# Own buffers for the first adaLN tiles, VectorE's copies in the paged units, and a unit's outputs turned within the late chunk

## The chip, the cores and the metric

One core of one Trainium2 chip runs the whole program in one launch. The metric is the device time of that launch in microseconds. A run gives one time; the profiled execution also gives a span, from the first to the last instruction of the program.

## The reference

Two decoder layers work on a prompt of 256 tokens and on 8 decoding sequences of 8 tokens with 1024 cached positions each (320 tokens, model width 1024, fp32). Cut to one layer:

```python
def run_layer(x, c, ...):
    sh, sc, g = adaln(c, w_ada_mix_l, b_ada_mix_l)      # silu(c) @ w + b, split in three
    h = x * (1 + sc) + sh
    o, state = mixer(split_heads(h @ w_in_l))
    x = layer_norm(DN_ALPHA * x + (1 + g) * (o @ w_o_l), ln1_g_l, ln1_b_l)
    sh, sc, g = adaln(c, w_ada_mlp_l, b_ada_mlp_l)
    h = x * (1 + sc) + sh
    f = jnp.square(jax.nn.relu(h @ w_up_l)) @ w_down_l
    x = layer_norm(DN_ALPHA * x + (1 + g) * f, ln2_g_l, ln2_b_l)
    return x, state
```

The mixer has three head groups: A (6 heads, dilated windows over a dense cache), B (6 heads, attention to the top 64 or 256 keys that an indexer of 8 small heads chooses, over a paged cache) and C (4 heads, the difference of two softmaxes, paged). A table of relative positions is added to the logits of all three.

## The kernel before, in words

**Tiles.** All weights but the indexer's own key matrix come as tiles of 128 x 1024 fp32 (512 KB). `STREAM` lists them in the order of use, `PLACE` gives each its number n, and tile n goes into slot n % 4 of `ring`. SyncE's `load` (L469) waits until tile n - 4 has been used (`tile_used`) and then issues one DMA.

**The front.** An adaLN row block is made from 4 tiles: `ada_tile` (PE, L1030) multiplies silu(c) by them into one PSUM bank, `ada_out` (ScalarE, L753) copies the bank to `adarow`, `ada_turn` (PE, L1040) transposes it, `ada_add` (VectorE, L1492 and on) adds groups and bias and writes `adaT`. `FIRST` is the shift (16 tiles' first half) and then the scale of layer 0, in order. After all 16 tiles VectorE makes h of the prompt (L1604, 8 instructions) and GpSimd h of the samples, and PE makes the indexer's queries: `by_chunks` (L1017, two tiles), two tiles by `chunk` (L1008), then keys and weights (L1084). On the way PE also makes a table of biases (L1060) that ScalarE stores to DRAM (L759), to be read back 16 times over by the bias loads. SyncE and ScalarE issue the 64 page loads of the indexer's cached keys (L489 and L774, 8 of 64 KB for each sequence); for each sequence the page numbers are read into registers first.

**Projections.** `PROJ` alternates dense tiles (8 of `feat`, 8 of `v`) with pairs of adaLN tiles. The indexer's scores come in between (`beside`), and from the seventh dense tile on VectorE takes the samples' top-k, 8 values at a time (`take8`: MAX8 L1593 and MATCH_REPLACE8 L1595), 32 times a layer.

**Attention.** 16 units follow: unit n is sequence n % 8, the first 8 with groups A and C, the last 8 (`second`) with B and C. Keys and values have two buffers each in `big`, so unit n + 2 is loaded when unit n is done with them: keys after its logits, values after its outputs. In a first unit the cache is 4 DMAs of 768 KB and 16 pages of 64 KB; in a second unit 8 + 8 pages of 192 KB and 8 + 8 of 64 KB, of which ScalarE issues the C keys (L873, 8) and SyncE the others (L489). Beside the units run 16 `item`s of the prompt's attention, about one per unit (`SLOTS`).

Within unit n PE does `turn(n)` (L1211, then a wait for `u_out` of unit n - 1, then L1220), `logits(n+1)` (L1192, in second units L1198 too), the item's transposes (L1280) and logits (L1265), `values(n)` (L1235), the item's outputs (L1290), a late weight chunk (L1008, in units 0 to 6), and `turn_out(n)` (L1242). ScalarE copies the turned weights out of PSUM (`turned_unit` L882 and L884, `turned_item` L901) and takes the exponentials (L840, L842, L893). VectorE reads logits (L1649, L1713), scales the unit's outputs (L1686 to L1690), scales the item (L1724, L1728), copies the item's outputs (L1742), takes one `take8`, puts the unit's outputs away (`place_outputs`, L1700, which signals `u_out`), and takes the other `take8` (units 0 to 6). After the 32nd, VectorE writes `sel` (L1782), for which the logits of unit 8 wait.

All orders are written by hand; nothing is scheduled by a planner.

## Time and profile before

| | us |
|---|---|
| runs shown, median (lowest, highest) | 1428.89 (1428.22, 1435.41) |
| the profiled execution's own time | 1424.0 |
| its span | 1422.2 |
| PE busy | 1298.5 (91%) |
| VectorE busy | 517.4 (36%) |
| ScalarE busy | 286.5 (20%) |
| GpSimd busy | 60.0 (4%) |
| moved by DMA | 363.79 MB, mean 256 GB/s |

In the table by stretch of time each engine has its busy time and, in brackets, its count of instructions; then come the share of full speed that TensorE's clock was granted and the mean busy share of the 16 DMA engines, where 1.00 and more is an engine set with no gap. In the timeline a row is a start, a length, engine and line, and in square brackets the engine's idle time before it with what ended it. SPq and ACTq are queues that issue DMAs. PEld is the weight load of PE.

### The profile page before, as it was taken

What the parts mean: (1) busy time and instruction counts of PE and PEld (TensorE: products, weight loads), DVE (VectorE), ACT (ScalarE), POOL (GpSimd) and SP (SyncE); (2) the same over time, 40 slices, a digit from 0 to 9 for tenths busy, and PEclk for the clock granted to TensorE, in tenths of its full rate; (3) what the DMA queues carried; (4) which work ended last, traced back from release to release, by engine and by line L of the source; (5) the groups of instructions that cost most, each with busy time, mean ns of one, the idle gap of its engine ahead of it and who ended that gap; (6) DMA issues with size and microseconds to landing.
All of it is one profiled execution on the core that took longest, in us unless ns stands there. A gap on an engine that the chain in (4) does not pass through costs nothing.

```text
span 1422.2 us, 23165 instructions
## 1 busy us (share of the span) xinstructions
PE 1298.5 (91%) x8038; PEld 814.3 (57%) x8038; DVE 517.4 (36%) x1350; ACT 286.5 (20%) x713; POOL 60.0 (4%) x265
## 2 busy tenths in 40 slices
PE   5789798878699999999999999998789999999998
PEld 1444255544466666666665544665456667767775
DVE  1102688865255111111113079777534611100113
ACT  0111123333223101100004112433322310100001
POOL 1100000000001000000001000000000100000000
PEclk9899999999899999999999999999979999999999
DMA  8778979999954667887864587999995446675663
GB/s 303 211 264 269 295 238 350 371 275 307 313 194 141 218 229 272 297 307 278 299 226 162 209 278 240 314 371 324 300 326 189 172 185 222 215 278 209 225 224 133
DMA packets 189565, 363.79 MB, mean 256 GB/s; under 512 B 22912, under 2 KB 140360, under 8 KB 187786
## 3 DMA queue, kind: packets, MB, share of 16 engines
q1 hardware_dynamic: 165200, 350.19, 71.9%
q10 hardware_dynamic: 24250, 12.14, 3.3%
q8 instruction: 64, 1.05, 0.3%
q14 instruction: 51, 0.42, 0.1%
HBM read 354.17 MB, written 58.40 MB: 290 GB/s over the span
## 4 chain that ended last, share of the span: by engine, by line
PE 70%; SPq 9%; DMA 7%; DVE 5%; issue 4%; DVEq 2%; ACT 2%; ACTq 0%
PE psf L1008 24%; PE psf L1424 19%; SPq L489 8%; DMA ring<-in_tiles 6%; PE psf L1300 4%; PE psf L1339 3%; PE psf L1407 3%; PE psf L1030 2%; PE psf L1235 2%; PE psf L1192 2%; PE psf L1079 1%; DVE m L1593 1%; DVEq L1596 1%; PE psf L1334 1%; PE psf L1105 1%
## 5 line engine op out<-in xcount | busy, mean ns | idle before, releaser
L1008 PE MATMUL psf<-hT,ring 128*128 128x320 f32 x1440 | 402.0, 437 | 11.1 <-DMA ring<-in_tiles 7.8
L1008 PEld LDWEIGHTS psf<-hT,ring 128*128 128x128 f32 x1440 | 271.5, 191 | 141.1 <-issue 14.7
L1424 PE MATMUL psf<-big,ring 128*128 128x320 f32 x1024 | 278.7, 433 | 3.8 <-DVE big L1811 2.1
L1424 PEld LDWEIGHTS psf<-big,ring 128*128 128x128 f32 x1024 | 193.5, 190 | 89.9 <-issue 5.8
L1811 DVE TENSOR_TENSOR big<-sq 128x320 f32<-128x320 f32 x64 | 31.5, 492 | 248.4 <-ACT sq L977 248.1
L1508 DVE TENSOR_SCALAR rstd<-psf,adaT 128x256 f32<-128x256 f32 x32 | 15.4, 482 | 248.9 <-PE psf L1424 233.7
L1192 PE MATMUL psf<-big,qs 128*32 128x512 f32 x512 | 74.6, 671 | 8.0 <-issue 5.6
L935 ACT ACTIVATE sq<-xT 128x320 f32<-128x320 f32 x32 | 15.0, 470 | 321.0 <-DVE xT L1512 321.0
L1593 DVE MAX8 m<-workbuf 64x8 f32<-64x1032 f32 x64 | 78.5, 1227 | 3.0
L1030 PE MATMUL psf<-ring,cz 128*32 128x512 f32 x384 | 61.8, 633 | 19.3 <-DMA ring<-in_tiles 10.7
L1595 DVE MATCH_REPLACE8 workbuf<-m,workbuf 64x1032 f32<-64x1032 f32 x64 | 77.4, 1209 | 0.0
L1235 PE MATMUL psf<-big,ptbuf 128*32 128x128 f32 x2048 | 66.1, 283 | 11.1 <-DMA big<-in_pool_cv 10.3
L977 ACT ACTIVATE sq<-psf 128x320 f32<-128x320 f32 x64 | 28.0, 437 | 238.9 <-PE psf L1008 224.5
L1300 PE MATMUL psf<-oT,ring 128*128 128x320 f32 x256 | 71.6, 435 | 2.1 <-DVE oT L1700 1.0
L1235 PEld LDWEIGHTS psf<-big,ptbuf 128*32 128x32 f32 x2048 | 57.2, 114 | 18.0 <-issue 16.2
L1649 DVE CUSTOM_DVE_ANT_0 S<-psf,sbias 128x1032 f32<-128x1032 f32 x32 | 39.4, 1233 | 60.4 <-PE psf L1198 54.6
L1300 PEld LDWEIGHTS psf<-oT,ring 128*128 128x128 f32 x256 | 47.8, 190 | 23.4 <-DVE xT L1512 1.7
L1339 PE MATMUL psf<-ring,hT 128*128 128x512 f32 x128 | 60.3, 615 | 0.0
L794 ACT ACTIVATE zT<-psf,zscale 128x320 f32<-128x320 f32 x40 | 20.7, 527 | 166.4 <-PE psf L1008 129.6
L1492 DVE TENSOR_REDUCE adaT<-psf 128x36 f32<-128x144 f32 x24 | 7.3, 304 | 117.3 <-PE psf L1040 116.8
L1220 PE MATMUL psf<-ident,S 128*128 128x128 f32 x128 | 22.4, 302 | 24.8 <-DVE oT L1700 24.3
L1407 PE MATMUL psf<-hT,big 128*128 128x320 f32 x128 | 38.3, 464 | 3.1 <-ACT hT L952 3.1
(183 smaller groups left out, 1158.8 us busy)
## 6 DMA issues: line engine op xcount, KB each, us to landing
ring<-in_tiles SPq DMA_DIRECT2D x284, 512.0 KB, 4.5
big<-in_cache_a SPq DMA_DIRECT2D x64, 768.0 KB, 7.2
out_cache_a<-in_cache_a SPq DMA_DIRECT2D x64, 768.0 KB, 5.8
big<-in_pool_bk SPq DMA_DIRECT2D x128, 192.0 KB, 3.7
big<-in_pool_bv SPq DMA_DIRECT2D x128, 192.0 KB, 4.6
big<-in_pool_cv SPq DMA_DIRECT2D x256, 64.0 KB, 4.3
big<-in_pool_ck SPq DMA_DIRECT2D x128, 64.0 KB, 4.4
big<-in_pool_ck ACTq DMA_DIRECT2D x128, 64.0 KB, 4.6
```

Of the source, the lines that this page charges most:

```text
L489: sp.dma_start(dst[:, j, :], pool[ds(at[j] + l * N_PHYS, 1), :, w0:w0 + dst.shape[2]] .rearrange("o p w -> (o p) w")).then_inc(signal, 16)
L1008: ins = pe.matmul(ps[:, 0:T], ring[:, s, k, :], rhs[:, k, :], start=k == 0, stop=k == KD - 1)
L1030: ins = pe.matmul(bank[3][G * g:G * g + G, :], cz[:, c, :], wide(s, kk), start=c < 4, stop=c >= 4)
L1192: ins = pe.matmul(psf[G * c:G * c + G, 512 * q:512 * q + w], qs[:, u.s, G * c:G * c + G], rhs, start=True, stop=not masked)
L1235: ins = pe.matmul(bank[3][G * c:G * c + G, 0:P], lhs, rhs, start=j == 0, stop=j == NPG)
L1300: ins = pe.matmul(wo_bank(m)[:, 0:T], ring[:, s, k, :], oT[:, AT_O[k], :], start=k == 0, stop=k == KD - 1)
L1339: ins = pe.matmul(bank[v_bank(g, tt)], hT[:, 2 * s + kk, P * tt:P * tt + P], wide(slot, kk), start=first, stop=last)
L1407: ins = pe.matmul(up_bank(m)[:, 0:T], spare[m][:, k, :], hT[:, k, :], start=k == 0, stop=k == KD - 1)
L1424: ins = pe.matmul(bank[6 + m % 2][:, 0:T], ring[:, s, k, :], uT[:, KD * q + k, :], start=q + k == 0, stop=q == 3 and k == KD - 1)
L1593: dve.max(m8[0:TS, 0, :], work)
L1595: dve.match_replace(work, m8[0:TS, 0, :], work, TAKEN)
L1649: dve.tensor_tensor_reduce(out=S[:, 0, :], in0=psf[:, 0:L], in1=sbias[u.second][:], scale=1.0, scalar=-3e38, op0=ALU.add, op1=ALU.max, acc ...
```

## The change

**Front.** `FIRST` takes the four groups of 4 tiles in the order 0, 2, 1, 3, so that shift and scale of chunks 0 to 3 come first. Only its first 4 tiles use the ring; the other 12 have buffers of their own (`ahead`, in `big` and in `zT`, both free then) and are issued without a wait. x goes behind 8 tiles, the four tiles of the indexer's queries go next into the ring, then the last 8 of FIRST. `ring_at` renumbers the slots. PE does half of the queries (chunks 0 to 3) behind the eighth tile and the other half behind the sixteenth; the bias table moves behind the twelfth. VectorE, GpSimd and ScalarE are put in the matching order, the small constants get two semaphores, and the indexer's page loads move: sequences 0 and 1 on SyncE ahead of the constants, 2 and 3 between the first projection tiles, and on ScalarE one sequence less at the start and one more behind the first tiles.

**A unit's outputs.** In units 0 to 6 `turn_out` stands between the halves of the late chunk, `place_outputs` stands ahead of both `take8`s. In units 7 to 14 `place_outputs` stands ahead of `item_out`. In units 13 and 14, which have another item, `turn_out` goes ahead of its steps.

**Paged units.** In the second units VectorE does the copies of `turned_unit` and `turned_item`, and ScalarE issues 4 of the 8 C value pages (`load_c_values`), behind a wait for the outputs of unit n.

```diff
-FIRST = some("mix", 0, 0, 16)
+FIRST = [t for q in (0, 2, 1, 3) for t in some("mix", 0, 4 * q, 4 * q + 4)]
...
+        ahead = [x.rearrange("p (k m) -> p k m", k=KD)
+                 for m in range(6) for x in (big[:, KD * P * (4 + m):KD * P * (5 + m)],
+                                             zT[:, :, :].rearrange("p z t -> p (z t)")[:, KD * P * m:KD * P * (m + 1)])]
...
+        def ring_at(t):
+
+            n = PLACE[t]
+            return n if n < RING else n - len(FIRST) + RING
...
             sp.dma_start(cT[:], a["cond"]).then_inc(ld_cond, 16)
-            for t in FIRST[:12]:
+            for t in FIRST[:RING]:
                 load(t)
+            for m in range(4):
+                load_ahead(m)
             sp.dma_start(xT[:], a["x"]).then_inc(ld_x, 16)
-            for t in FIRST[12:]:
+            for t in INDEX[0]:
                 load(t)
+            for m in range(4, 12):
+                load_ahead(m)
...
                     sp.wait_ge(ld_first, N_FIRST)
-                    load_ik(l, 0)
+                    for b in range(2):
+                        load_ik(l, b)
...
                     load(t)
+                    if l == 0 and n in (1, 3):
+                        load_ik(l, 2 + n // 2)
...
-                    load_c(l, then, was, 1)
+                    load_c(l, then, was, 1, range(NPG // 2 if then.second else NPG))
...
             for n, t in enumerate(FIRST):
                 ada_tile(t)
-                if n == 3:
+                if n == 4:
+                    pe.wait_ge(ld_begin, N_BEGIN)
+                    ada_turn(0)
+                if n in (7, 11):
+                    ada_turn(n // 4)
+                if n == 7:
+                    for m, q in enumerate(INDEX[0]):
+                        part_of_queries(m, q, range(KD // 2))
+                if n == 11:
                     pe.wait_ge(ld_first, N_FIRST)
...
-                    by_chunks(l, 0, INDEX[l][:2], in_bank)
-                    for m in range(2, 4):
-                        chunk(INDEX[l][m], in_bank(m), hT)
+                    for m, q in enumerate(INDEX[l]):
+                        part_of_queries(m, q, range(KD // 2, KD)).then_inc(tile_used, 1)
...
-                        chunk(MID[l][u.n + 1], late_bank(u.n + 1), hT)
+                        late = MID[l][u.n + 1]
+                        part_of_chunk(late, late_bank(u.n + 1), range(KD // 2))
+                        turn_out(u)
+                        part_of_chunk(late, late_bank(u.n + 1), range(KD // 2, KD)).then_inc(tile_used, 1)
+                    else:
+                        turn_out(u)
                     for k in slots[1:]:
                         item_turn(k - 1)
                         item_logits(k)
-                    turn_out(u)
-                    for k in slots[1:]:
                         item_outputs(k - 1)
...
+                    if NB <= u.n + 2 < UNITS:
+
+                        act.wait_ge(u_o.sem, u_o.done(l, u.n))
+                        load_c_values(UNIT[u.n + 2], was)
...
                 for u in UNIT[:-1]:
                     n, slots = u.n, SLOTS[u.n]
+                    if u.second:
+                        turned_unit(u)
                     read_logits(UNIT[n + 1])
+                    if u.second:
+                        turned_item(slots[0] - 1)
                     item_read(slots[0])
                     read_outputs(u)
                     item_scale(slots[0])
+                    if n + 1 >= len(LATE):
+                        place_outputs(u)
                     if slots[0]:
                         item_out(slots[0] - 1)
+                    if n + 1 < len(LATE):
+                        place_outputs(u)
...
-                    while taken < upto - 1:
-                        take8()
-                        taken += 1
-                    place_outputs(u)
```

On PE, at the start of the program, the order before is this (L1030 adaLN tiles, L1040 their transposes, L1017 and L1008 the queries, L1084 the indexer's keys):

```order
L1040 MATMUL psf<-ident,adarow 128x128 x4
L1030 MATMUL psf<-ring,cz 32x512 x8
L1040 MATMUL psf<-ident,adarow 128x128 x4
L1030 MATMUL psf<-ring,cz 32x512 x6
L1040 MATMUL psf<-ident,adarow 128x128 x4
L1017 MATMUL psf<-hT,ring 128x320 x16
L1008 MATMUL psf<-hT,ring 128x320 x16
L1084 MATMUL psf<-hT,wki 72x320 x8
L1008 MATMUL psf<-hT,ring 128x320 x8
```

In the same place it is now (L1073 adaLN tiles, L1083 transposes, L1103 the queries, L1120 the bias table, L1140 the indexer's keys, L1056 the first projection):

```order
L1083 MATMUL psf<-ident,adarow 128x128 x4
L1103 MATMUL psf<-hT,ring 128x320 x16
L1073 MATMUL psf<-big,cz 32x512 x2
L1073 MATMUL psf<-zT,cz 32x512 x2
L1073 MATMUL psf<-big,cz 32x512 x2
L1073 MATMUL psf<-zT,cz 32x512 x2
L1083 MATMUL psf<-ident,adarow 128x128 x4
L1120 MATMUL psf<-big,relb 16x512 x2
...
L1083 MATMUL psf<-ident,adarow 128x128 x4
L1103 MATMUL psf<-hT,ring 128x320 x16
L1140 MATMUL psf<-hT,wki 72x320 x8
L1056 MATMUL psf<-hT,ring 128x320 x8
```

The first 16 of the queries' 32 matrix products now stand ahead of the last 8 adaLN tiles, and the bias table behind four of these.

On PE, within unit 1 of a layer, from the unit's last value product on, it was (L1242 is `turn_out`, L1220 the transposes that wait for `u_out`):

```order
L1235 MATMUL psf<-vs,ptbuf 32x128 x4
L1290 MATMUL psf<-adarow,vp 64x128 [waits i_tset]
L1290 MATMUL psf<-adarow,vp 64x128
L1008 MATMUL psf<-hT,ring 128x320 [waits ld_w2,i_logit]
L1008 MATMUL psf<-hT,ring 128x320 x7
L1242 MATMUL psf<-turnO,osb 128x64 [waits u_oset]
L1211 MATMUL psf<-ident,S 128x128 [waits u_exp,u_tset]
L1211 MATMUL psf<-ident,S 128x128 x3
L1212 MATMUL psf<-ident,znew 64x128
L1220 MATMUL psf<-ident,S 128x128 [waits u_out]
```

and is now:

```order
L1363 MATMUL psf<-hT,ring 128x320 [waits ld_w2,i_logit]
L1363 MATMUL psf<-hT,ring 128x320 x3
L1298 MATMUL psf<-turnO,osb 128x64 [waits u_oset]
L1363 MATMUL psf<-hT,ring 128x320 [waits ld_w2]
L1363 MATMUL psf<-hT,ring 128x320 x3
L1267 MATMUL psf<-ident,S 128x128 [waits u_exp,u_tset]
L1267 MATMUL psf<-ident,S 128x128 x3
L1268 MATMUL psf<-ident,znew 64x128
L1276 MATMUL psf<-ident,S 128x128 [waits u_out]
```

`turn_out` moved ahead by half a chunk, and so stands farther from the transposes that wait for what comes of it.

On VectorE, at the start of unit 8, the first paged unit, the order now is (L1839 and L1841 are `turned_unit`, L1724 the logits of unit 9, L1849 `turned_item`):

```order
L1839 COPY ptbuf<-psf 64x128 [waits u_o,u_tp]
L1841 COPY ptbuf<-psf 128x512 x2
L1724 ISA S,mx<-psf,sbias 128x1032 [waits u_s,u_tp]
L1724 ISA mx 128x1
L1727 TENSOR_SCALAR nmx<-mx 128x1
L1849 COPY adarow<-psf 128x512 [waits i_o,i_tp]
L1788 ISA S,mxi<-psf,pbias 128x128 [waits i_s,i_tp]
```

Before, the row of L1649 (now L1724) was the unit's first on VectorE and L1713 (now L1788) followed its two helpers; the four copies stood on ScalarE.

## Rows read from the trace of the kernel before

**Rows 1.** Windows: stretch, length, busy (count) by engine, PE clock, DMA share, GB/s.

```profile
0.00:38.60 38.60, 20.32 (x86) 4.73 (x86) 7.46 (x30) 4.03 (x7) 5.67 (x18) 0.95 0.84 306
38.60:68.70 30.10, 23.32 (x80) 15.28 (x80) 2.93 (x7) 3.07 (x7) 3.40 (x10) 0.90 0.74 189
68.70:100.00 31.30, 27.51 (x108) 15.32 (x108) 0.46 (x3) 3.29 (x6) 0.00 (x0) 0.89 0.84 276
212.00:300.00 88.00, 76.87 (x856) 50.05 (x858) 72.81 (x196) 31.29 (x90) 6.78 (x36) 0.99 1.03 353
300.00:305.00 5.00, 5.00 (x103) 3.14 (x95) 2.34 (x8) 1.62 (x4) 1.13 (x6) 0.88 0.33 96
320.00:377.00 57.00, 42.08 (x571) 26.08 (x571) 25.08 (x101) 20.94 (x61) 4.52 (x24) 0.91 1.01 313
377.00:403.00 26.00, 22.16 (x265) 14.84 (x269) 9.21 (x39) 9.60 (x26) 0.00 (x0) 0.87 0.81 265
895.00:980.00 85.00, 76.10 (x858) 50.13 (x861) 68.04 (x192) 32.00 (x93) 6.78 (x36) 1.00 1.05 361
980.00:990.00 10.00, 8.16 (x141) 5.02 (x137) 6.17 (x25) 3.41 (x11) 1.13 (x6) 1.00 0.84 248
```

**Rows 2.** Timeline of PE, 0 to 100 us.

```profile
13.48 2.12 PE L1060 MATMUL psf<-big,relb 34*16 34x512 f32 x6 [1.26 <-DMA zscale<-in_zscale]
...
23.20 1.05 PE L1030 MATMUL psf<-ring,cz 128*32 128x512 f32 x4 [1.27 <-DMA ring<-in_tiles]
24.50 1.05 PE L1030 MATMUL psf<-ring,cz 128*32 128x512 f32 x4 [0.24 <-DMA ring<-in_tiles]
...
36.17 0.66 PE L1040 MATMUL psf<-ident,adarow 128*128 128x128 f32 x4 [0.70 <-ACT adarow L753]
38.63 10.40 PE L1017 MATMUL psf<-hT,ring 128*128 128x320 f32 x32 [1.80 <-DVE hT L1604]
48.86 8.78 PE L1008 MATMUL psf<-hT,ring 128*128 128x320 f32 x32
57.48 4.47 PE L1084 MATMUL psf<-hT,wki 128*72 128x320 f32 x16
68.73 6.41 PE L1008 MATMUL psf<-hT,ring 128*128 128x320 f32 x16 [6.79 <-DMA ring<-in_tiles]
...
91.32 1.05 PE L1030 MATMUL psf<-ring,cz 128*32 128x512 f32 x4 [3.09 <-DMA ring<-in_tiles]
```

**Rows 3.** Timeline of PEld and VectorE, 0 to 40 us.

```profile
11.17 0.14 PEld L1030 LDWEIGHTS psf<-ring,cz 128*32 128x32 f32 x4 [0.98 <-DMA ring<-in_tiles]
...
37.54 3.99 DVE L1604 TENSOR_SCALAR hT<-xT,adaT 128x256 f32<-128x256 f32 x8
```

**Rows 4.** Timeline of SyncE's queue, 35 to 70 us.

```profile
40.48 11.96 SPq L489 DMA_DIRECT2D big<-in_pool_ik  x8
```

**Rows 5.** Waits, 205 to 296 us (layer 0, units 0 to 7): total, times, longest.

```profile
PE psf L1220 <- DVE oT L1700: 4.5, 4, 2.0
```

**Rows 6.** Waits, 296 to 405 us (layer 0, units 8 to 15).

```profile
PE psf L1220 <- DVE oT L1700: 8.4, 7, 2.8
...
PE psf L1235 <- DMA big<-in_pool_cv: 6.4, 2, 4.7
```

**Rows 7.** Waits, 975 to 1085 us (layer 1, units 8 to 15).

```profile
PE psf L1235 <- DMA big<-in_pool_cv: 3.9, 2, 2.5
```

**Rows 8.** Groups by shape, VectorE's and ScalarE's: busy us, mean ns, idle before.

```profile
L1664 DVE COPY workbuf<-psf 64x512 f32<-64x512 f32 x4 | 2.8, 688 | 11.2 <-PEq L1119 11.1
...
L884 ACT ACTIVATE ptbuf<-psf 128x512 f32<-128x512 f32 x64 | 34.0, 582 | 0.0
```

**Rows 9.** VectorE, 296 to 405 us: its groups by shape, then its timeline.

```profile
L1742 DVE COPY oT<-psf 64x128 f32<-64x128 f32 x18 | 5.1, 286 | 0.2
...
313.05 1.23 DVE L1649 CUSTOM_DVE_ANT_0 S<-psf,sbias 128x1032 f32<-128x1032 f32 x1 [3.50 <-PE psf L1198]
```

**Rows 10.** Timeline of SyncE's queue, 356 to 402 us.

```profile
369.35 4.02 SPq L489 DMA_DIRECT2D big<-in_pool_cv  x8
```

205 lines of the change are left out of this document (126 added, 79 removed).

## The prediction, made before the changed kernel was run

> **What bounds the kernel now.** I read the windows first, since the whole-span shares hide that three places have three limits. The reader is to look at the last two columns, DMA share and GB/s. In the front the 16 DMA engines are busy 0.84, 0.74 and 0.84 of three stretches that cover 0 to 100 us; in the units of layer 0 the share is 1.03 over 88 us and in the paged units 1.01, and the same of layer 1 (1.05) [rows 1]. So in the attention DMA sets the pace and in the front it should, but doesn't. Then the timeline of PE over the front. Three things stand there. From 17 to 30 us every adaLN product waits for its tile: starts at 23.20 and 24.50, 1.30 apart, each only 1.05 long [rows 2]. From 36 to 62 us the work is PE's own, in a row: h, 10.40, 8.78, 4.47 [rows 2]; the DMA share falls to 0.74 there because the four ring slots hold the tiles in use. And at 68.73 PE has stood 6.79 us for the first projection tile, then runs it at 6.41 [rows 2]. The queue of SyncE tells why: its eight page loads of one sequence took 11.96 us to issue, from 40.48 to 52.44 [rows 4], with the constants, another eight and the first projection tiles behind them. Last the waits in the units: PE stood for `place_outputs` 4.5 us in units 0 to 7 and 8.4 us in units 8 to 15 [rows 5, 6], and for C values 6.4 us there [rows 6] and 3.9 us in layer 1 [rows 7].
>
> **The sum is made against the profiled execution's own 1424.0 us** (span 1422.2). The median of the runs shown is 4.9 above it, so 4.9 is added at the end.
>
> **Front, the tiles.** The third ring tile behind the first came in at 11.17 [rows 3]. From there at 1.30 a tile, twelve buffers of their own, no wait: the eighth tile (4 more) at 16.4, x, 1280 KB or 2.5 tiles, at 19.6, the four query tiles from 20.9 to 24.8, the last of the 16 at 24.8 + 8 x 1.30 = 35.2.
>
> **Front, PE.** Behind the eighth tile: its product 1.05, the copy to `adarow` 0.58 (ScalarE's 582 ns for 128 x 512 out of PSUM [rows 8]), the transposes 0.66, VectorE's add, taken at 0.5, and the first chunk of h, 3.99 / 8 = 0.5 [rows 3], so the queries begin near 20.1, by when x is in. Half of the queries is half of 10.40 + 8.78, taken warm at 8.8; the last two of the four query tiles come at 23.5 and 24.8, ahead of their use. So to about 29. Then four adaLN products, 4.2, copy 0.6, transposes 0.66 and the bias table 2.12 [rows 2]: 37 to 38, by which all tiles are in (35.2). Four products 4.2 to 41.9; copy, transposes, add and h with nothing beside them, 0.6 + 0.66 + 0.5 + 0.5, to 44.2; the second half 8.8 to 53.0; keys 4.47 to 57.5. Before, that chain ended at 57.48 + 4.47 = 61.95. **4.5 us** of PE's own chain go: the adaLN pieces between the halves are paid, the idle tile waits aren't.
>
> **Front, the first projection.** The query tiles' slots come free only with the second half (about 46 to 53), but slots 0 to 3 hold just those four: the first projection tile needs the first query tile's slot, so it leaves at about 47 and has 10 us to land. A 512 KB tile at the pace above is 1.3, and SyncE's page loads now stand in front of it, two sequences (16 issues; at the worst rate seen 24 us, at the rate of another eight, 4.02 us [rows 10], 8 us). They are issued right behind the last ahead tile at about 25 to 30, long before 47, where nothing on SyncE waits for a slot. Two more sequences stand between projection tiles, 4 to 12 us of issuing each in front of the third and fifth tile; the low end keeps a loss of that kind. I take the wait of 6.79 as gone, and with it the cold chunk: 6.41 against 8.78 / 2 = 4.39 warm, 2.0. So far 4.5 + 6.8 + 2.0 = 13.3. At 91.32 PE waited 3.09 for an adaLN tile [rows 2]; with the queue ahead of it relieved perhaps all of it goes and about 1.5 of slower products behind, 4.6: 17.9 in all.
>
> **What caps it.** DMA work does not shrink. 38.6 x 0.84 + 30.1 x 0.74 + 31.3 x 0.84 = 81 us of work stand in the first 100 [rows 1]. At a share of 0.97, about 83.6 us: at most 16.4 can go. At its start the queue is empty and can't reach that share. I take **14** for the front; low end 7 (only the chain's 4.5 and half the cold and waiting time less a new queue wait), high end 17.
>
> **Front, edits at nothing.** The smaller first semaphore (`ld_begin`), the lambda exponential moved behind the second copy, h in halves on GpSimd: all run beside tile waits. The bias table's store leaves ScalarE about 42 instead of about 20; the bias loads that wait for it stand behind the fourth projection tile on SyncE, due past 60. If that cover is gone, every tile behind that wait is late by the store's own length.
>
> **Units 0 to 7.** `turn_out` half a chunk (about 2.2 us) earlier removes what stood as 4.5 us in four waits [rows 5]. Moved are one transposition pair on PE and two copies on VectorE; the two `take8` ahead of which they now stand are late by these copies, 2 x 0.286 us at most, the row of a copy four times as wide [rows 9], and the last of them frees `sel`, for which unit 8's logits wait: 0.6 once a layer. But the DMA share there is 1.03 [rows 1]: a unit that ends 0.6 us earlier frees its keys earlier, and the transfer for n + 2 is still queued behind others. What is real is the gap: at 300 to 305 the share is 0.33, 0.67 x 5 = 3.35 us of empty DMA [rows 1], where unit 8 waits for `sel` and the keys and values of 9 and 10 can't leave. An earlier end of unit 7 moves the whole gap, and shortens it only if DMA finished its queue earlier too. Bounds: 0 and 4.5.
>
> **Paged units.** Per unit VectorE gets one small copy, 0.286 [rows 9], and two of 128 x 512, 2 x 0.688, together 1.66 us, and the item's, between 0.286 and 0.688 by its width, 0.55 in the mean; that size on VectorE is not in the trace with 128 partitions, the nearest row is 688 ns for 512 elements of 64 partitions; ScalarE took 582 [rows 8]. They stand in front of VectorE's read of the next logits, ahead of which it now stands idle for 3.50 us, waiting for PE's logits [rows 9]; 1.66 fits in there, so they are covered; the item's copy is in front of nothing that is ready. ScalarE gives up about 2 us of copies and gets four issues, 4.02 / 8 = 0.50 each [rows 10], 2.0 us, at a wait for `u_o`. Queued behind this wait is only the next unit's exponentials, not ready before. SyncE loses the same 2.0 us of 16 issues, eight of which took 4.02 [rows 10]. The share of 1.01 over 320:377 gives nothing to win; from 377 to 403 it is 0.81 [rows 1], an empty 0.19 x 26 = 4.9 us, with the longest C value wait, 4.7 [rows 6], in it. There half of the pages leave earlier: 2 to 3 us. With a share of the 3.35 at the gap, and about 1 to 2 of the units' own waits, **6** for layer 0 (0 to 13).
>
> The Trainium skill, *DMA: Bandwidth & Descriptors*, "Issuing engines are not separate DMA queues", says that DMAs started by several engines run on the same 16 and save the starting time of the sequencer only. By it the four issues that move to ScalarE are worth nothing where the trace shows a share of 1.01, and at most 4 x 0.5 us a unit in the tail. The trace of before agrees as far as it goes: cache loads already leave from two queues and the share is not above that of units with one.
>
> **Layer 1.** Share 1.05 over 85 us, then a gap of 0.16 x 10 = 1.6 us [rows 1], C value waits 3.9, longest 2.5 [rows 7]. I take **3** (0 to 6).
>
> **Sum.** 14 + 6 + 3 = 23: 1424.0 − 23 = 1401.0, and 4.9 for the median, **1406**.
>
> **Rivals.**
> (a) *Only the front counts*: the attention is DMA's in both layers, and PE merely waits for keys instead of for `u_out`. For it: shares of 1.03, 1.01, 1.05. Against: the gap at 300 and the tail at 377. 14 to 15: about **1414**.
> (b) *The front gives half*: page loads, constants and the bias store now share the saturated engines with the ahead tiles; at 11.96 for eight issues [rows 4], two sequences would hold SyncE up to 24 us, from 30 to 54, and the first projection tile, free at 47, leaves at 54. The 6.8 is then still about half there. 7 + 9 for the units: about **1413**.
> (c) *More*: the front at its cap 17 and the units' waits really gone, 4.5 + 3 in layer 0's first units, 5 in its tail, and half as much in layer 1, 33: about **1396**.
> (d) *The change does not do what it says*: ahead tiles land later since 12 tiles compete with page loads, x and constants; the halves each wait, and nothing within 0.5% remains: **1426**.
> (e) *Slower: VectorE's copies come on the path of the paged units.* PE transposes, VectorE copies, and PE's values can't start till then. If VectorE is still in the earlier unit's `item_out`, `place_outputs` or a top-k step, the copies end behind the logits. It decides from the point where that idle time ahead of the read, 3.50, is under the copies' own 1.66: then 14 units x (1.66 + 0.55) = 31 us are on the path, less 14 of the front: about **1446**. Against it: VectorE is busy 25 of 57 us there [rows 1].
> The Trainium skill, *VectorE: DVE Perf Modes*, "The TRN2 errata", has a table by which a copy of 512 out of PSUM takes (120 + 512) cycles at 0.96 GHz, 658 ns, on VectorE and (172 + 512) at 1.2 GHz, 570 ns, on ScalarE. The rows, 688 and 582, say the same with a little more: the engine to which the copies move is the slower one for them. That speaks against this part, and it matters only in (e).
>
> **Chances.** Forecast 0.56, (a) 0.17, (b) 0.10, (c) 0.07, (d) 0.06, (e) 0.04. A measurement of this kernel can tell about 0.5%, 7.1 us, from no change: faster than 1421.8 are the forecast, (a), (b) and (c), 0.90; same (d), 0.06; slower (e), 0.04. The range leaves out (d) and (e), and a tenth more on its two sides: 1393 to 1420. Its low end is all terms at their high ends (17 + 13 + 6 = 36), its high end the front's low end of 7 with 2 for the units.
>
> **What would show it.** The first projection chunk starts at 57 to 60 instead of 68.73 and has no long DMA wait; if it waits still for a ring tile behind page loads, (b). PE's waits for `place_outputs` shrink to under 1 us in units 0 to 7; if then waits for keys grow by as much, (a). The DMA share in the five us ahead of unit 9 rises from 0.33, and the longest C value wait falls from 4.7. VectorE's copies in the paged units end before PE's logits do; if a wait of the value products for VectorE stands among the waits with 1 us and more a unit, (e). The front's DMA share is 0.95 over 10 to 60 us. I am wrong if the share there stays at 0.8 with every tile in a buffer of its own, or if the stage between 100 and 212 us, which I left alone, stretches by what the front gave.

## The result and the profile after

| | before | after |
|---|---|---|
| median of the runs (lowest, highest), us | 1429.41 (1428.22, 1435.41) | 1408.67 (1405.41, 1411.64) |
| span of the profiled execution, us | 1422.2 | 1409.6 |
| VectorE busy, us | 517.4 | 550.2 |
| ScalarE busy, us | 286.5 | 258.1 |
| mean rate of DMA, GB/s | 256 | 258 |

The ratio (time of the changed kernel over that of before) is 0.9846, with a 95% interval of 0.981 to 0.9882: 22 us less (0.0154 x 1429; the two medians are 20.7 apart), where 23 was forecast. A second measurement of the same kernel gave 0.9854 (0.9821 to 0.9887). The two profiled executions are only 12.6 us apart: of before the profiled one was a quick one. A single trace stands for its kernel's median to about 5 us here, and in the runs below to about 8. Below, us of a part are always (1 − ratio) x 1429; the intervals are about 4 us to either side.

The forecast had 14 us for the front and 9 for the units. The parts measured alone (next section) came out otherwise, and the profile after already hints at it. The timeline of PE in the front of the changed kernel (start, length, engine and line, idle time before in brackets; L1103 queries, L1140 the indexer's keys, L1056 projection tiles):

```profile
24.01 8.85 PE L1103 MATMUL psf<-hT,ring 128*128 128x320 f32 x32 [1.88 <-DVE hT L1547]
...
42.99 10.54 PE L1103 MATMUL psf<-hT,ring 128*128 128x320 f32 x32 [1.80 <-DVE hT L1547]
53.37 4.47 PE L1140 MATMUL psf<-hT,wki 128*72 128x320 f32 x16
59.97 6.26 PE L1056 MATMUL psf<-hT,ring 128*128 128x320 f32 x16 [2.13 <-DMA ring<-in_tiles]
...
77.83 7.60 PE L1056 MATMUL psf<-hT,ring 128*128 128x320 f32 x16 [5.61 <-DMA ring<-in_tiles]
```

Against [rows 2] the first projection tile starts at 59.97 instead of 68.73 after a wait of 2.13 instead of 6.79. The wait at 91.32 is gone, but one of 5.61 stands at 77.83. Why the tiles were late is in the queue of SyncE, same kernel (L499 own-buffer tiles, L519 page loads, L584 constants, L493 ring tiles):

```profile
26.75 15.12 SPq L519 DMA_DIRECT2D big<-in_pool_ik  x16
41.92 4.76 SPq L584 DMA_DIRECT2D ident<-in_ident  x1
46.72 4.67 SPq L584 DMA_DIRECT2D onesd<-in_onesd  x1
...
55.59 1.06 SPq L493 DMA_DIRECT2D ring<-in_tiles  x2
59.68 3.96 SPq L519 DMA_DIRECT2D big<-in_pool_ik  x8
63.69 0.90 SPq L493 DMA_DIRECT2D ring<-in_tiles  x2
67.44 4.33 SPq L519 DMA_DIRECT2D big<-in_pool_ik  x8
...
72.23 0.36 SPq L493 DMA_DIRECT2D ring<-in_tiles  x1
```

The first projection tile leaves at 55.59, not at 47 as the prediction had it, since two constants took 4.7 us each to issue; the fifth leaves at 72.23, behind page loads, though the tile whose slot it takes was used by 66.2. The first of the two waits comes back in a second trace of the same kernel, the second only in part:

```profile
61.66 7.52 PE L1056 MATMUL psf<-hT,ring 128*128 128x320 f32 x16 [3.01 <-DMA ring<-in_tiles]
...
77.72 6.24 PE L1056 MATMUL psf<-hT,ring 128*128 128x320 f32 x16 [2.55 <-DMA ring<-in_tiles]
```

What filled the DMA engines meanwhile shows in the windows of the kernel after (length, busy by engine, PE clock, DMA share, GB/s) and in ScalarE's queue, first of before, then of after:

```profile
40.00:45.00 5.00, 2.67 (x8) 1.87 (x9) 3.25 (x13) 0.48 (x1) 1.64 (x4) 0.80 0.89 123
45.00:50.00 5.00, 5.00 (x17) 3.38 (x17) 0.62 (x5) 0.00 (x0) 0.00 (x0) 0.85 0.99 105
```

```profile
35.53 0.68 ACTq L759 DMA_DIRECT2D dist_sample<-big  x1
```

```profile
39.89 0.67 ACTq L795 DMA_DIRECT2D dist_sample<-big  x1
```

A share of 0.99 at 105 GB/s is the bias table's store: 16 partitions x 16 repeated rows of 4.6 KB, 1.19 MB. From 42 to 46 us of this trace the store's queue took 97% of the engines' time for 0.40 MB in 87 packets, so of 4.6 KB each; the page loads that run at 350 GB/s in the units have packets of 0.9 KB. Small packets are thus not what makes the store slow, and no run shows what does. It ran ahead of the constants before, and runs into them now. What it ran beside before were page loads: the 11.96 us for eight in [rows 4], which the prediction used as a worst rate, stand mostly under it (it landed at 50.4) and beside 16 page loads of ScalarE.

In the units, PE's waits for `place_outputs` in units 0 to 7 are gone, and another has come. The waits of PE from 205 to 292 us of the kernel after (total, times, longest); this is the only row there, and below it the row of before for the same helper, which stood there beside that of [rows 5]:

```profile
PE psf L1363 <- DVE nmxi L1793: 7.9, 7, 1.7
```

```profile
PE psf L1008 <- DVE nmxi L1718: 1.0, 2, 0.7
```

L1363 is the first half of the late chunk, which waits until VectorE has read the item's logits, since it takes their bank. And in the paged units the windows read differently from [rows 1]; here of the kernel after:

```profile
310.00:370.00 60.00, 47.12 (x654) 28.38 (x654) 37.37 (x134) 14.03 (x48) 4.54 (x24) 0.92 1.10 350
370.00:405.00 35.00, 32.14 (x286) 21.43 (x287) 18.76 (x59) 5.76 (x15) 0.00 (x0) 0.84 0.61 202
```

A share of 1.10 and 350 GB/s stand where before stood 1.01 and 313: the stage that I had called full was not. It is the same in layer 1, from 990 to 1050 us: 1.01 and 314 before, 1.10 and 352 after.

### The profile page after: what moved, and what is told of

It reads as the page before. It is cut to its first block, busy times and chain, and to the rows that moved or that the text cites. A ratio compares the mean times of both kernels' runs of the same rounds, so it can differ in the third digit from the quotient of the medians.

```text
span 1409.6 us, 23104 instructions
## 1 busy us (share of the span) xinstructions
PE 1297.3 (92%) x8038; PEld 815.8 (58%) x8038; DVE 550.2 (39%) x1416; ACT 258.1 (18%) x647; POOL 60.2 (4%) x265
## 3 DMA queue, kind: packets, MB, share of 16 engines
q8 instruction: 64, 1.05, 0.3%
## 4 chain that ended last, share of the span: by engine, by line
PE 65%; SPq 10%; DVE 8%; DMA 6%; DVEq 4%; issue 4%; ACT 2%; ACTq 0%
PE psf L1056 22%; PE psf L1490 18%; SPq L519 8%; DMA ring<-in_tiles 5%; PE psf L1356 4%; PE psf L1402 3%; DVEq L1676 3%; DVE m L1673 3%; PE psf L1473 3%; PE psf L1073 2%; PE psf L1135 1%; DMA big<-in_pool_cv 1%; PE psf L1291 1%; DVE S L1724 1%; PE psf L1248 1%
## 5 line engine op out<-in xcount | busy, mean ns | idle before, releaser
L1056 PE MATMUL psf<-hT,ring 128*128 128x320 f32 x1184 | 331.3, 439 | 8.8 <-DMA ring<-in_tiles 8.5
L1056 PEld LDWEIGHTS psf<-hT,ring 128*128 128x128 f32 x1184 | 225.2, 192 | 118.0 <-issue 21.1
L1363 PE MATMUL psf<-hT,ring 128*128 128x320 f32 x224 | 67.1, 442 | 13.3 <-DVE nmxi L1793 13.3
L1402 PE MATMUL psf<-ring,hT 128*128 128x512 f32 x128 | 63.8, 644 | 0.0
L1291 PEld LDWEIGHTS psf<-big,ptbuf 128*32 128x32 f32 x2048 | 55.0, 111 | 13.9 <-issue 12.0
L1073 PE MATMUL psf<-ring,cz 128*32 128x512 f32 x336 | 49.1, 624 | 10.4 <-DVE cz L1524 8.7
L1363 PEld LDWEIGHTS psf<-hT,ring 128*128 128x128 f32 x224 | 40.3, 190 | 29.9 <-DVE nmxi L1793 16.2
L1724 DVE CUSTOM_DVE_ANT_0 S<-psf,sbias 128x1032 f32<-128x1032 f32 x32 | 39.4, 1231 | 32.2 <-PE psf L1254 24.2
L829 ACT ACTIVATE zT<-psf,zscale 128x320 f32<-128x320 f32 x40 | 20.7, 528 | 165.7 <-PE psf L1056 85.2
```

The lines of the kernel that those rows point to most:

```text
L1056: ins = pe.matmul(ps[:, 0:T], ring[:, s, k, :], rhs[:, k, :], start=k == 0, stop=k == KD - 1)
L1073: ins = pe.matmul(bank[3][G * g:G * g + G, :], cz[:, c, :], wide(tile, kk), start=c < 4, stop=c >= 4)
L1291: ins = pe.matmul(bank[3][G * c:G * c + G, 0:P], lhs, rhs, start=j == 0, stop=j == NPG)
L1363: ins = pe.matmul(ps[:, 0:T], ring[:, s, k, :], hT[:, k, :], start=k == 0, stop=k == KD - 1)
L1402: ins = pe.matmul(bank[v_bank(g, tt)], hT[:, 2 * s + kk, P * tt:P * tt + P], wide(ring[:, slot], kk), start=first, stop=last)
L1724: dve.tensor_tensor_reduce(out=S[:, 0, :], in0=psf[:, 0:L], in1=sbias[u.second][:], scale=1.0, scalar=-3e38, op0=ALU.add, op1=ALU.max, acc ...
```

## Experiments

**The whole, and its parts.** First the whole again, the front alone, and everything but the front. The front alone is the kernel before with the first part of the change and nothing of the others.

> The whole change once more, as the measure for the parts. The median of its runs was 1408.7 us against 1429.4 before, 20.7 less; in the two profiled executions the spans differ by only 12.6. Both theories: 1405 to 1411, 18 to 24 less than before.

> The front alone: own buffers, half of the queries behind the eighth tile, page loads moved. Theory A (the sum of the prediction): 14 us less than before, 1415. Theory B (what the two traces show at the first unit's value products, 208.5 before and 205.5 after): the first projection tiles come sooner, but a later one waits 5.6 us behind page loads, so 3 to 7 us less, 1422 to 1426.

> Everything but the front: the outputs turned within the late chunk, VectorE's copies, ScalarE's value loads. Theory A: 9 us less than before, 1420. Theory B (from the traces, the units of layer 0 give 6.6 us and those of layer 1 4.6, with some of it lost in between): 10 to 14 us less, 1415 to 1419. A rival C, that front and units hide each other since both only move work ahead of the same transfers: each alone gives nearly the whole 20 us.

| kernel | median, us | ratio (interval) | less than before |
|---|---|---|---|
| whole | 1407.72 | 0.9854 (0.9821, 0.9887) | 20.9 |
| front only | 1423.00 | 0.9953 (0.9927, 0.9979) | 6.7 |
| units only | 1415.34 | 0.9905 (0.9869, 0.994) | 13.6 |

6.7 + 13.6 = 20.3 against 20.9: the parts add up, and rival C falls (each alone nearly 20). The front is worth 7, half of what the prediction gave it; theory B holds. Does it arrive, or is it lost on the way? The start of PE's value products in three units, of before and then of the front alone (only the starts are to be read; length and count stop where the stretch asked for stops):

```profile
208.53 0.74 PE L1235 MATMUL psf<-big,ptbuf 128*32 128x128 f32 x18
...
402.56 1.19 PE L1235 MATMUL psf<-big,ptbuf 128*32 128x128 f32 x36
...
1081.67 1.08 PE L1235 MATMUL psf<-big,ptbuf 128*32 128x128 f32 x32
```

```profile
200.23 0.97 PE L1278 MATMUL psf<-big,ptbuf 128*32 128x128 f32 x28
...
397.51 0.75 PE L1278 MATMUL psf<-big,ptbuf 128*32 128x128 f32 x20
...
1081.17 1.08 PE L1278 MATMUL psf<-big,ptbuf 128*32 128x128 f32 x32
```

8.3 us ahead at the first unit of layer 0, 5.1 at its last, 0.5 at the last of layer 1. But one pair can't tell loss from scatter, and the traces of the other runs of this document can be put beside it. At the first unit, the four kernels with the old front start at 207.3 to 212.5, mean 208.9; those with this front, eight traces, at 199.5 to 205.5, mean 201.9. That is 7.0 apart, as much as the front is worth in time. At about 100 us (the dense tile that starts at 105.14 before and 98.68 after) the two means are 105.8 and 97.9, 7.8 apart. So the front gains 8 where it was made, not 14, and most of it is there when the units begin. Behind them single pairs differ too much: 0.5 to 4 us at the last unit of layer 1 in the three pairs of kernels that differ by the front alone.

**The third part, taken out.** In the paged units ScalarE copies and SyncE issues all values, as before; front and outputs stay. Of the edit, one line of SyncE and one of ScalarE:

```diff
-                    load_c(l, then, was, 1, range(NPG // 2 if then.second else NPG))
+                    load_c(l, then, was, 1)
...
-                    if not u.second:
-                        turned_unit(u)
+                    turned_unit(u)
```

> The change without its third part: in the paged units ScalarE copies and SyncE issues all C values, as before. Theory A (tail of layer 0 2 to 3 us, layer 1 up to 3): 4 to 6 us slower than the whole change, 1413 to 1415. Theory B (in the trace the step between the units 11 and 12 gives 4.4 us in layer 0 and 3.2 in layer 1, both where PE waited for C values): 7 to 9 us slower, 1416 to 1418. If VectorE's copies cost what the value loads give, no difference.

1418.01 us, ratio 0.9926 (0.9898 to 0.9954): 10.6 less than before, so 10.3 above the whole (4 to 16 with both intervals). That is nearer to theory B, and on the far side of it from the prediction's 4 to 6. This small part is half of the change.

**Its two halves, and the second part taken out.** These ran beside other runs of before, with a median of 1426.33; only ratios are compared.

The first without the early outputs:

```diff
-                        part_of_chunk(late, late_bank(u.n + 1), range(KD // 2))
-                        turn_out(u)
-                        part_of_chunk(late, late_bank(u.n + 1), range(KD // 2, KD)).then_inc(tile_used, 1)
+                        part_of_chunk(late, late_bank(u.n + 1), range(KD)).then_inc(tile_used, 1)
```

> The change without its second part: turn_out and place_outputs stand where they stood before. The whole change had 1407.7, the parts so far: front 6.4, paged part 10.3, which leaves 21.6 - 16.7 = 4.9 for this part. Theory A (additive): 1411 to 1414. Rival (the transposes' waits for oT were hidden by DMA that is busy all the time, as in the rival of the prediction in which only the front counts): no difference, 1406 to 1409.

The second with the copies of the paged units on ScalarE, here VectorE's side:

```diff
-                    if u.second:
-                        turned_unit(u)
                     read_logits(UNIT[n + 1])
-                    if u.second:
-                        turned_item(slots[0] - 1)
```

> The change, but in the paged units ScalarE copies the turned weights again; it still issues 4 of the 8 C value pages. Of the paged part's 10.3 us, theory A (the copies only make room on ScalarE for the issues; they cost nothing and give nothing by themselves, but with both on ScalarE its queue is late): 2 to 5 us slower than the whole, 1410 to 1413. Theory B (the gain is the loads' alone): no difference, 1406 to 1409. Theory C (the copies are on the path and VectorE is quicker to them, since ScalarE still takes exponentials): the larger part of the 10, 1414 to 1418.

The third with all 8 value pages on SyncE, here ScalarE's side:

```diff
-                    if NB <= u.n + 2 < UNITS:
-                        act.wait_ge(u_o.sem, u_o.done(l, u.n))
-                        load_c_values(UNIT[u.n + 2], was)
```

> The change, but SyncE issues all 8 C value pages; VectorE copies. Theory A and B: the gain is in the issues, 6 to 10 us slower than the whole, 1414 to 1418. Theory C: 0 to 3 us slower.

| front and outputs, and in the paged units | ratio (interval) | less than before |
|---|---|---|
| neither (the run above) | 0.9926 (0.9898, 0.9954) | 10.6 |
| value loads on ScalarE, copies there too | 0.9901 (0.9867, 0.9934) | 14.1 |
| copies on VectorE, loads on SyncE | 0.9948 (0.9928, 0.9968) | 7.4 |
| both | 0.9854 (0.9821, 0.9887) | 20.9 |
| both, without the early outputs | 0.9879 (0.9852, 0.9907) | 17.3 |

On top of front and outputs the copies alone bring nothing (7.4 against 10.6, intervals that overlap), the loads alone 3.5 (interval −3 to 10, so not told from nothing), both together 10.3: 13.5 us separate both from the copies alone, well outside the intervals (8 to 19), where 6 to 10 was expected of that run. What the copies are for shows in the waits of PE with loads and copies both on ScalarE, 286 to 402 us:

```profile
PE psf L1248 <- ACT ptbuf L924: 5.3, 4, 2.3
```

PE's next logits wait for ScalarE's copy, which stands in its queue behind the issues and their wait for `u_o`; in the trace of the whole there is no such row. SyncE's queue then waits for PE in turn, 300 to 385 us, which it does in neither trace of the whole:

```profile
SPq L519 <- PE psf L1291: 2.6, 1, 2.6
```

So theory A of that run is borne out in its mechanism; its size, 6.8 us, has an interval of 0 to 13 us when those of both runs are put together.

The run without the early outputs is 3.6 us above the whole, inside its interval: inconclusive by itself. The part alone settled more.

**The second part alone.**

> The kernel before, with the second part alone: turn_out between the halves of the late chunk, place_outputs earlier. Theory A (its waits were real, 4.9 us were left for it by the other parts): 3 to 6 us less than before, 1421 to 1425. Theory B (the share of DMA is 1.03 in units 0 to 7, so what PE gains it waits for keys; the change without this part came out 3.5 us above the whole, within its interval): 0 to 2 us less, 1425 to 1428.

1426.19 us against 1426.85, ratio 0.9993 (0.9966 to 1.0021): nothing that can be told from no change, theory B in its number. Its reason, waits for keys, is not what PE's waits show, though. The waits of PE in this kernel, 205 to 296 us:

```profile
PE psf L1315 <- DVE nmxi L1736: 7.0, 6, 1.5
```

Before there were 4.5 us for `oT` [rows 5] and 1.0 for `nmxi` in two waits; now 7.0 for `nmxi`. PE comes to the late chunk sooner and stands there for VectorE's read of the item's logits. VectorE is busy 72.8 of 88 us in these units [rows 1]: what it does was put in another order, none of it was taken away, and PE waits for it at another place. Those two rows of waits grew from 5.5 to 7.0 us together.

**The value loads alone**, on top of the kernel before:

```diff
-                    load_c(l, then, was, 1)
+                    load_c(l, then, was, 1, range(NPG // 2 if then.second else NPG))
...
+                    if NB <= u.n + 2 < UNITS:
+                        act.wait_ge(u_o.sem, u_o.done(l, u.n))
+                        load_c_values(UNIT[u.n + 2], was)
```

> The kernel before, with one edit: in the paged units ScalarE issues 4 of the 8 C value pages behind the wait for the outputs of unit n. Measured so far, against before: neither loads nor VectorE's copies (but front and outputs) -10.6 us, loads alone with these -14.1, copies alone -7.4, both -20.9. Theory A (two queues move more than one: in the traces of the paged units the 16 engines move 349 to 354 GB/s at a share of 1.10 with the loads on ScalarE, 307 to 320 at 1.00 to 1.02 without): the rate between 340 and 370 us rises from 305 to 340 or more, and 3 to 8 us less than before, 1419 to 1424. Theory B (only the tail of a layer's units gains, by issue time, 4 x 0.5 us a unit there): rate as before, 0 to 4 us less, 1423 to 1427.

1414.08 us against 1426.85, ratio 0.9916 (0.9883 to 0.9949): 12.0 less (7 to 17), where theory A gave 3 to 8. One edit that adds no work and removes none brings about half of the change. It brings more here than the 3.5 that it brought above, with ScalarE doing the copies in both; the difference of 8.5 has an interval of 1 to 16, and no run explains it. The windows from 310 to 370 us: this kernel; then the change with SyncE issuing all; then the second part alone, which has all on SyncE too; then the loads on ScalarE with the copies there too, on top of front and outputs; each from its own trace.

```profile
310.00:370.00 60.00, 47.71 (x713) 28.97 (x717) 29.98 (x123) 24.77 (x75) 5.64 (x30) 0.97 1.10 349
```

```profile
310.00:370.00 60.00, 44.38 (x572) 26.67 (x571) 36.41 (x129) 13.36 (x44) 4.51 (x24) 0.89 1.00 317
```

```profile
310.00:370.00 60.00, 46.90 (x666) 29.29 (x666) 30.05 (x125) 23.69 (x71) 5.64 (x30) 0.91 1.00 308
```

```profile
310.00:370.00 60.00, 48.46 (x680) 27.85 (x672) 30.03 (x123) 21.61 (x64) 4.52 (x24) 0.94 1.05 335
```

The five kernels with all values on SyncE move 304 to 317 GB/s there, seven with ScalarE's loads 349 to 352. The last row is the exception: there SyncE's queue stood for PE, as shown above.

**Bytes or issues?** Theory A of that run spoke of two queues moving more. The next run has as many issues on each queue as the whole change, but three times the bytes in those that ScalarE has:

```diff
-                        act.dma_start(cv_in[u.s][:, j, :],
-                                      a["pool_cv"][ds(at[j] + l * N_PHYS, 1), :, P:2 * P].rearrange("o p w -> (o p) w")
-                                      ).then_inc(ld_cv[u.s], 16)
+                        act.dma_start(v_in[u.s][:, j, :],
+                                      a["pool_bv"][ds(at[j] + l * N_PHYS, 1), :, :].rearrange("o p w -> (o p) w")
+                                      ).then_inc(ld_v[u.s], 16)
```

> The change, but ScalarE issues 4 of the 8 B value pages (192 KB each) in place of 4 of the 8 C value pages (64 KB); SyncE issues all C values. As many issues on each engine, three times the bytes on the second queue. Theory A (two queues fill the DMA engines better, by the bytes on the second): the rate in the paged units is at least that of the whole change (350 GB/s), 1400 to 1407. Theory B (it is the issue time on SyncE alone): equal issues, equal time, 1405 to 1409. Rival C (the last load of a unit sets its start, and that is C's, now all behind B's on SyncE): slower, 1410 to 1416.

1407.70 us, ratio 0.9863 (0.9836 to 0.9891), the whole's within the interval, so rival C falls; the window from 310 to 370 us:

```profile
310.00:370.00 60.00, 45.56 (x647) 28.57 (x651) 37.60 (x135) 15.08 (x53) 4.56 (x24) 0.94 1.10 351
```

The same rate and the same time with the same number of issues. By itself this can't refuse theory A, since the whole's 350 GB/s may be all that the engines give, whatever the queues. What settles it is SyncE's own queue from 310 to 370 us, of before, of the whole and of this kernel (packets, MB, share of the 16 engines):

```profile
q1 hardware_dynamic: 14132, 15.44, 81.3%
```

```profile
q1 hardware_dynamic: 13543, 17.03, 84.6%
```

```profile
q1 hardware_dynamic: 12999, 13.71, 70.1%
```

Before and in the whole it issued 100 loads in these 60 us, but moved 15.44 MB with them before and 17.03 in the whole. So it was not at a limit of bytes; what stayed the same is the count of issues. Its rows show how it was spent. Of before, then of after, one paged unit after the other:

```profile
316.07 5.20 SPq L489 DMA_DIRECT2D big<-in_pool_bk  x8
321.37 4.04 SPq L489 DMA_DIRECT2D big<-in_pool_bv  x8
325.62 4.66 SPq L489 DMA_DIRECT2D big<-in_pool_cv  x8
331.10 3.95 SPq L489 DMA_DIRECT2D big<-in_pool_bk  x8
```

```profile
320.86 4.72 SPq L519 DMA_DIRECT2D big<-in_pool_bk  x8
325.68 3.75 SPq L519 DMA_DIRECT2D big<-in_pool_bv  x8
329.62 2.87 SPq L519 DMA_DIRECT2D big<-in_pool_cv  x4
333.30 3.95 SPq L519 DMA_DIRECT2D big<-in_pool_bk  x8
```

Before, the queue never rests: from 316.07 to 331.10 it issues 13.9 of 15.0 us, and in the rest, 1.1, the program has it read the next page numbers; it waits for no engine between 302 and 375. At the 0.50 of [rows 10] 24 issues are 24 x 0.50 = 12.0 us and the reading 1.1, 13.1 a unit. A unit is (8 + 8) x 192 + (8 + 8) x 64 KB = 4.19 MB, so by this estimate SyncE can ask for about 4.19 MB / 13.1 us = 320 GB/s, and 317 is what the change with all on SyncE moved. With 20 issues it is 10.0 + 1.1 = 11.1 us, and now the engines at 350 GB/s need 12.0 for a unit; the queue goes round in 12.4 (320.86 to 333.30). That the engines are the bound now is an estimate from these sums: the queue doesn't rest after either (11.3 us of issuing in that round). For it speaks that a B value page takes longer from issue to landing, median 5.1 us before, 6.9 in the whole:

```profile
big<-in_pool_bv SPq DMA_DIRECT2D x33, 192.0 KB, 5.1
```

```profile
big<-in_pool_bv SPq DMA_DIRECT2D x43, 192.0 KB, 6.9
```

The Trainium skill, *Perfetto Trace Analysis*, "Identifying the Most-Contended Engine", advises HBM utilization in place of occupancy for DMA, because 16 engines make occupancy misleading, and under "DMA Optimizations" that balancing over the issuing engines may help where making the descriptors is the bottleneck and the issuing engine looks busy. Both agree with this case: the share read 1.01 at 313 GB/s before, where 1.10 and 350 were to be had, and SyncE was issuing 13.9 of 15.0 us.

**The front, mended.** Two kernels asked whether the front's missing half can be had. The first puts two projection tiles ahead of the constants and moves page loads behind:

```diff
-                    sp.wait_ge(zeroed, 2)
-                    for dst, src in consts:
-                        sp.dma_start(dst, src).then_inc(ld_const, 16)
                 at, d = None, 0
                 for n, t in enumerate(PROJ[l]):
                     load(t)
-                    if l == 0 and n in (1, 3):
-                        load_ik(l, 2 + n // 2)
+                    if l == 0 and n == 1:
+                        sp.wait_ge(zeroed, 2)
+                        for dst, src in consts:
+                            sp.dma_start(dst, src).then_inc(ld_const, 16)
+                    if l == 0 and n in (2, 5):
+                        load_ik(l, 2 + n // 4)
```

> The change with another order on SyncE in the front: the first two projection tiles ahead of the nine constants, and the page loads of the sequences 2 and 3 behind the third and the sixth projection tile instead of the second and the fourth. In the trace of the change the first projection waits 2.1 us and the third dense tile 5.6 us for tiles that stood behind these. Theory A (SyncE's order sets both waits): both shrink, 4 to 7 us at the first unit's value products, and 2 to 6 us in the time, 1402 to 1406. Rival (the 16 DMA engines are full there from the bias store, which moves 1.2 MB in small pieces from 40 to 54 us, so that the order changes nothing): the waits move, 1406 to 1409.

1405.03 us, ratio 0.9858 (0.9835 to 0.9882): as the whole. The local effect is there; PE's timeline of this kernel:

```profile
61.22 4.47 PE L1057 MATMUL psf<-hT,ring 128*128 128x320 f32 x16
...
73.67 1.91 PE L1074 MATMUL psf<-ring,cz 128*32 128x512 f32 x4 [2.01 <-DMA ring<-in_tiles]
```

The first projection doesn't wait, and its chunk takes 4.47 us instead of 6.26 and 7.52. The second wait is 2.0, against 5.61 and 2.55 in the two traces of the whole. At the first unit's value products this kernel is at 199.5, within the 199.5 to 205.5 of the kernels without the edit; the 4 to 7 us of theory A are not there. In the time nothing of it can be told.

The second also halves the store ahead of the samples' bias loads:

```diff
-            act.dma_start(dist_s, bass.AP(distb.tensor, distb.offset,
-                          [list(distb.ap[0]), [0, REP], [1, NDIST]])).then_inc(st_dist, 16)
+            def store_dist(half, signal):
+
+                act.dma_start(dist_s[:, NT * half:NT * half + NT, :], bass.AP(distb.tensor, distb.offset,
+                              [list(distb.ap[0]), [0, NT], [1, NDIST]])).then_inc(signal, 16)
+
+            store_dist(0, st_dist)
...
+                    if l == 0 and n == 1:
+                        store_dist(1, st_rest)
```

> As e8 (the first two projection tiles ahead of the constants, page loads later), and the bias table's store in two: the first 8 of the 16 repeated rows where the store stood, which is all that the samples' bias loads read, the other 8 behind ScalarE's last page loads at about 80 us, from a buffer of its own. Theory A (the store fills the 16 engines from 40 to 54 us at 105 to 125 GB/s and holds up SyncE's queue, where two issues took 4.7 us each): the store's first half lands 6 to 7 us sooner, no issue above 2 us on SyncE behind 47 us, the first unit's value products 2 to 5 us sooner than in e8 measured from the front's own start, and the time 0 to 5 us less than e8, 1400 to 1405, since part of what the front gives is lost again before the end of the units. Rival (the queue is slow for page loads, not for the store): the issues stay at 4.7 us and the time at e8's, 1404 to 1408.

1406.55 us, ratio 0.9866 (0.9829 to 0.9903). PE's timeline and ScalarE's queue of this kernel:

```profile
59.45 4.47 PE L1066 MATMUL psf<-hT,ring 128*128 128x320 f32 x16
...
83.21 1.92 PE L1083 MATMUL psf<-ring,cz 128*32 128x512 f32 x4 [4.18 <-DMA ring<-in_tiles]
```

```profile
41.84 0.35 ACTq L801 DMA_DIRECT2D dist_sample<-pbias  x1
...
81.82 0.47 ACTq L801 DMA_DIRECT2D dist_sample<-pbias  x1
```

The queue of SyncE behaves as theory A says: its two ring tiles at 48.88 take 2.49 us together (4.84 at 50.65 without the split). The constants behind them take at most 0.57 with and without it, so they say nothing. PE now waits 4.18 us ahead of 83.21. That is not the other half of the store, issued at 81.82, when the wait was nearly over; the tile waited for, by its place in the order, left at 77.08, behind eight page loads that this kernel has there:

```profile
72.28 4.35 SPq L520 DMA_DIRECT2D big<-in_pool_ik  x8
...
77.08 0.37 SPq L494 DMA_DIRECT2D ring<-in_tiles  x1
```

That the store holds up the queue is shown; that anything is gained in time by splitting it is not.

## Why the prediction was right, and where it was right by chance

The time, 1406 forecast and 1408.7 measured, and the range hold. The composition doesn't: 14 + 9 was forecast, 7 + 14 came. Two steps failed in opposite directions, and that they cancelled is luck.

- **Front, PE's chain**: forecast ends of 57.5 for the indexer's keys, measured 53.37 + 4.47 = 57.84. The first projection was to start at 57 to 60 and started at 59.97. Right in its end, by two errors that cancelled. The eighth tile's product ended at 20.8 instead of 17.5, and the queries began at 24.0 instead of 20.1. But the two groups of four adaLN products took 1.9 us each (32.80 to 34.71, 37.87 to 39.79), not 4.2: 1.05 a tile was their length where each waited for its tile. The second half of the queries began at 42.99, 1.2 us sooner than forecast, and took 10.54 instead of 8.8, behind a wait for h of 1.80 (granted clock 0.80 and 0.85 there).
- **Front, the first projection**: the step that failed. "SyncE's page loads ... are issued at about 25 to 30, long before 47" held for their start alone: they took 15.12 us, to 41.9, and the constants behind them until 55.6. I had put a price on the page loads and none on the constants. The wait is 2.13 and the chunk cold, 6.26. The second half of the term, 4.6 for the wait at 91.32, was met by a new 5.61 and 7.60 − 4.57 = 3.0 of slower products at 77.83. Step by step in this trace, the chain's end is 4.1 us ahead of before, the first projection chunk's end 8.9, the third dense chunk's end 0.2 (85.43 against 85.63), the chunk at 98.68 6.5. Both losses are rival (b)'s mechanism, and 7 for the front was its price. The page loads were slow (0.95 us each) while the ahead tiles came in at 400 GB/s beside them for most of that time, as (b) has it; the constants were slow beside the store.
- **Front, edits at nothing**: wrong in a premise. The store of the bias table did not leave at about 20 us before, but at 35.53; the cover was thinner than I wrote, and the store (0.99 share at 105 GB/s) is what the constants ran into. Its cover on the bias loads held: they left from 71.8 on, and the store had landed at 53.6.
- **What caps it**: the cap of 16.4 took busy share for work. The share over 10 to 60 us came out at 0.94, as the 0.95 forecast, and the front still gave half: 0.99 of it stood beside 105 GB/s. "No gap", as the text ahead of the prediction calls 1.00, is not "nothing left": 1.00 at 309 GB/s before, from 310 to 370 us, left room for 350.
- **Units 0 to 7**: "removes what stood as 4.5 us": it does, and 6 to 7 us of waits for VectorE's `nmxi` come in. Bounds 0 and 4.5, measured 1.0 +- 4 for the part alone. The reason that I gave, DMA, is not the one that the waits show. The gap ahead of unit 9 didn't close either: 0.37 at 98 GB/s from 295 to 300 us of after, against 0.33 at 96 from 300 to 305 before.
- **Paged units**: the step that failed most, "the share of 1.01 over 320:377 gives nothing to win". The row itself said 313 GB/s beside 353 of [rows 1]; I read the share and not the rate beside it. I had the 0.50 of an issue too, and priced four of them, out of 16; SyncE had 24 a unit, and these, 12 us, I never set against the 13.7 to 16.1 us of a round. The part gives 10.3, the loads alone 12.0, against the 2 to 3 a layer that I gave them.
- **The rule of the Trainium skill on issuing engines**, *DMA: Bandwidth & Descriptors*, "Issuing engines are not separate DMA queues", says that a second issuing engine saves only issuing time. The runs agree (100 issues on SyncE in 60 us before and in the whole, equal time with equal issues); its remark that this time is usually small doesn't fit here, where issuing took 13.9 of 15.0 us. What I drew from it, worth nothing where the share is 1.01, was wrong, because issuing was the bound there.
- **VectorE's copies**: priced rightly (0.673 and 0.283 us each where 0.688 and 0.286 were taken) and covered, as said; PE has no wait for VectorE's copies among its waits in the paged units of after, and rival (e) didn't come. What they are good for I hadn't seen: with the value loads on ScalarE, copies made there stand on PE's path (5.3 us of waits).
- **Rivals**: (a), only the front counts, is refuted: the front alone is 6.7. (b) was right for the front, and its 9 for the units too low. (c) and (d) didn't come. In (c) the terms as listed, 17 + 12.5 and half of 12.5 again, make 36 and not 33.
- **The stage between 100 and 212 us**, named as a sign of being wrong if it stretched, took 103.1 us on average with the old front and 104.0 with the new, from the dense tile near 100 us to the first unit's value products: it gave back about 1 of 8.

Open: whether any of the front's 7 us at the first unit is lost behind it, whether the early outputs are worth the 3.6 us by which the kernel without them was slower, why the loads alone brought 12.0 on the kernel before and 3.5 on front and outputs, and why the store moves so little.

## What to carry to other kernels

Where many small loads keep a stage busy, count the issues: issues a round x time of one, plus the reading of addresses, against the round. Where that sum was the round, the other edits of the units brought nothing that could be measured, and moving a sixth of the issues to another queue brought 12 us (7 to 17). Before calling a stage full by its busy share, compare its rate with the best rate in the same trace. And a wait that vanishes from the table is no gain until the sum of the waits of that engine has shrunk.

## What was not expected of the hardware

- The busy share of the 16 DMA engines reads 0.99 to 1.01 at 304 to 317 GB/s and 1.10 to 1.11 at 349 to 352 in the same stage, 310 to 370 us; at 45 to 50 us it reads 0.99 at 105 GB/s. Here it was no measure of what is left.
- One issue of a page load on SyncE takes 0.46 to 0.50 us where nothing held it up (3.7 to 4.0 for 8). One issue of a constant took up to 4.8 us while the bias table's store was under way, and 0.36 to 0.57 in the kernel before, where the store was over by then.
- A store of 16 partitions x 16 rows of 4.6 KB (1.19 MB) ran at about 87 GB/s, from 39.9 to 53.6 us; half of it took 7.4. Its packets of 4.6 KB are larger than the 0.9 KB of the page loads that ran at 350.
